# Normed rows kept in natural order; TensorE and GpSimd read them with a step of eight

## What is computed

```
x  = x + g1 * (merged @ w_out)                        # out-projection and residual
h2 = rms_norm(x, norm2_g) * (1.0 + sc2) + sh2         # the normed rows of this case
logits = h2 @ w_router + b_router                     # 32 experts, the best 4 of each token
act = clamp/SwiGLU(h2[tokens of e] @ w_gu[e] + b_gu[e])
y[tokens of e] += weight * (act @ w_down[e] + b_down[e])
x  = x + g2 * y ;  out = rms_norm(x, final_g)
```

## Time and profile before

| | |
|---|---|
| median of 3 executions | 937.23 us (936.38 to 937.92) |
| the profiled execution's own time | 932.74 us |
| its span, first to last instruction | 931.0 us |
| TensorE busy | 895.7 us (96%) |
| TensorE weight loads | 525.3 us (56%) |
| VectorE, ScalarE, GpSimd busy | 454.4, 180.2, 250.0 us |
| mean granted clock of TensorE | 0.994 |
| DMA | 283.75 MB, mean 305 GB/s |

### The profile page before, as it was taken

The page is one execution under the profiler, slowest core; times in us unless marked ns, Lnnn a source line. Parts: engine busy times, 40 slices in busy tenths (PEclk is TensorE's granted clock), DMA queues, the critical chain, the costliest instruction groups (busy, mean ns, idle before and its releaser), DMA issues.

```text
span 931.0 us, 22683 instructions
## 1 busy us (share of the span) xinstructions
PE 895.7 (96%) x10115; PEld 525.3 (56%) x10115; DVE 454.4 (49%) x946; ACT 180.2 (19%) x361; POOL 250.0 (27%) x248
## 2 busy tenths in 40 slices
PE   3999999999999998989999999999999999999994
PEld 2676756766788755755545454544545454544551
DVE  0389967544633556754352534344352534344355
ACT  6344454544322414100000000000000000000012
POOL 2333952202400003223223131323223131323102
PEclk9999999999999999999999999999999999999998
DMA  9937554305422967679999999999999999999965
GB/s 322 366 130 271 181 173 157 123 1 198 175 96 79 408 259 293 257 301 354 375 407 390 407 399 402 404 399 407 394 409 395 409 397 407 404 402 408 391 246 195
DMA packets 64124, 283.75 MB, mean 305 GB/s; under 512 B 7428, under 2 KB 9052, under 8 KB 39448
## 3 DMA queue, kind: packets, MB, share of 16 engines
q1 hardware_dynamic: 53528, 257.93, 69.8%
q0 software_dynamic: 10496, 24.32, 9.3%
HBM read 271.83 MB, written 18.50 MB: 312 GB/s over the span
## 4 chain that ended last, share of the span: by engine, by line
PE 84%; DVE 9%; ACT 3%; DMA 2%; issue 1%; SPq 0%; DVEq 0%; ACTq 0%; POOLq 0%
PE ps L1859 36%; PE ps L1578 16%; PE ps L1882 12%; PE ps L1872 6%; PE ps L1813 2%; DVE small L1157 2%; DVE top L1156 2%; PE ps L1632 2%; PE ps L1718 2%; PE ps L1853 2%; PE ps L1599 1%; DMA moe_rows<-X 1%; PE ps L1733 1%; DVE small L1142 1%; DMA X<-in_x_dram 1%
## 5 line engine op out<-in xcount | busy, mean ns | idle before, releaser
L1354 DVE TENSOR_SCALAR mix<-ps 128x384 f32<-128x384 f32 x32 | 17.9, 558 | 280.1 <-ACT attn L1019 280.1
L753 POOL DMA_INDIRECT moe_rows<-mix,idx x31 | 45.9, 1482 | 345.6 <-DVE mix L1412 345.6
L1578 PE MATMUL ps<-h_hi,wb_hl 128*128 128x512 f32 x384 | 125.5, 400 | 0.0
L1019 ACT ACTIVATE attn<-ps 128x384 f32<-128x384 f32 x32 | 15.7, 491 | 493.2 <-PE ps L1859 493.2
L747 POOL DMA_INDIRECT apad<-h_rows,idx x93 | 97.3, 1046 | 50.6 <-issue 27.7
L1578 PEld LDWEIGHTS ps<-h_hi,wb_hl 128*128 128x128 f32 x384 | 72.1, 188 | 20.8 <-issue 3.9
L1859 PE MATMUL ps<-ring,mix 128*32 128x256 f32 x1440 | 80.0, 379 | 0.0
L1859 PE MATMUL ps<-ring,uvp 128*32 128x256 f32 x1344 | 76.3, 383 | 0.0
L1578 PE MATMUL ps<-h_lo,wb_hl 128*128 128x512 f32 x192 | 74.8, 390 | 0.0
L1404 DVE SCALAR_TENSOR_TENSOR mix<-ps,WC,attn 32x256 f32<-32x256 f32 x128 | 61.6, 481 | 3.8 <-PE ps L1872 1.4
L1859 PEld LDWEIGHTS ps<-ring,mix 128*32 128x32 f32 x1440 | 43.0, 110 | 33.1
(11 more groups left out here) (312 smaller groups left out, 1346.7 us busy)
## 6 DMA issues: line engine op xcount, KB each, us to landing
ring<-in_w_gu_dram SPq DMA_DIRECT2D x58, 1024.0 KB, 23.8
ring<-in_w_down_dram SPq DMA_DIRECT2D x30, 1024.0 KB, 25.7
ring<-in_w_ada_dram SPq DMA_DIRECT2D x12, 2048.0 KB, 11.2
area_b<-in_w_gu_dram SPq DMA_DIRECT2D x17, 1024.0 KB, 18.9
hT<-in_w_gu_dram SPq DMA_DIRECT2D x17, 1024.0 KB, 22.9
area_a<-in_w_gu_dram SPq DMA_DIRECT2D x15, 1024.0 KB, 23.7
X<-in_w_gu_dram SPq DMA_DIRECT2D x14, 1024.0 KB, 26.1
ring<-in_w_in_dram SPq DMA_DIRECT2D x6, 2048.0 KB, 9.1
```

What stands on the lines that cost most here:

```text
L753: pool.indirect_dma_start(out=y_dram, in_=Y[0:slots, b, :], in_offset=None, out_offset=bass.IndirectOffsetOnAxis(ap=which, axis=0), bounds ...
L1578: last = mm(out_, a, b, start=(n == 0 and start_), stop=(n == len(pairs) - 1))
```

## The change

The normed rows are left in the order of X. VectorE's two operations are both in plain order, `first` moves to another tile, and the readers take the step of eight: TensorE's transposes and its product for expert 0 take every eighth element of a row as a block of weights, and GpSimd's copy reads with the same step. Chunk 2's normed row lies in `uvp` and no longer in X, chunk 3's still in `apad`; both are made in place, with no use of the scratch tile. The wait for `y_begun` remains for chunks 0 and 1 and is gone for chunk 2.

```diff
-        h2 = [X[:, ch, :] for ch in range(C - 1)] + [apad_flat[:, PG * (PAD + T) - D:PG * (PAD + T)]]
+        h2 = [X[:, 0, :], X[:, 1, :], uvp[:, :, :].rearrange("p a t -> p (a t)"),
+              apad_flat[:, PG * (PAD + T) - D:PG * (PAD + T)]]
+        h2_block = [t.rearrange("p (q k) -> p k q", k=KD) for t in h2]
...
-        first = natural[:, 0:C * slots].rearrange("p (c s) -> p c s", c=C)
+        first = mix[:, 3072:3072 + C * slots].rearrange("p (c s) -> p c s", c=C)
...
                 nc.gpsimd.tensor_copy(staged[ch % 2].rearrange("p (a k f) -> p k a f", a=NQ, k=KD),
-                                      h2[ch].rearrange("p (k a f) -> p k a f", a=NQ, k=KD)).then_inc(staged_ok, 1)
+                                      h2[ch].rearrange("p (a f k) -> p k a f", a=NQ, k=KD)).then_inc(staged_ok, 1)
...
-            def by_k(row):
-                return row.rearrange("p (q k) -> p k q", k=KD)
...
             def h2_rows(ch):
                 dve.wait_ge(ss3_ok, ch + 1)
                 link(v.reciprocal(rstd3[:, ch:ch + 1], ss3[:, ch:ch + 1]))
-                link(v.scalar_tensor_tensor(out=natural, in0=X[:, ch, :], scalar=rstd3[:, ch:ch + 1], in1=A2b,
+                scaled = natural if ch < 2 else h2[ch]
+                if ch == C - 1:
+                    dve.wait_ge(xg_clear, 1)
+                link(v.scalar_tensor_tensor(out=scaled, in0=X[:, ch, :], scalar=rstd3[:, ch:ch + 1], in1=A2b,
                                             op0=ALU.mult, op1=ALU.mult))
-                if ch < C - 1:
+                if ch < 2:
                     dve.wait_ge(y_begun[ch], 16)
-                else:
-                    dve.wait_ge(xg_clear, 1)
-                v.tensor_tensor(h2[ch].rearrange("p (k q) -> p k q", k=KD), by_k(natural), by_k(sh2b),
-                                ALU.add).then_inc(h2_ok, 1)
+                v.tensor_tensor(h2[ch], scaled, sh2b, ALU.add).then_inc(h2_ok, 1)
...
                     for k in range(4):
-                        at = (4 * half + k) * P
-                        last = nc.tensor.transpose(b_[:, k * P:(k + 1) * P], h2[ch][:, at:at + P], ident[:, :])
+                        last = nc.tensor.transpose(b_[:, k * P:(k + 1) * P], h2_block[ch][:, 4 * half + k, :], ident[:, :])
...
-                    last = mm(ps[:, 4 + k // 4, (k % 4) * P:(k % 4) * P + slots], h2[ch][:, k * P:(k + 1) * P], first[:, ch, :],
+                    last = mm(ps[:, 4 + k // 4, (k % 4) * P:(k % 4) * P + slots], h2_block[ch][:, k, :], first[:, ch, :],
```

## The result

The changed kernel takes 947.55 us (median of 4 executions, 946.77 to 947.86), the kernel before on the same chip 936.81 us (4 executions, 934.65 to 937.92). The ratio is 1.0119, with a 95% interval of 1.0103 to 1.0134: slower, by about 11.1 us by the ratio and 10.7 by the two medians. The profiled execution took 947.52 us; its span is 945.4 us, for 931.0 before.

The account below looks back on a forecast made before the run. TensorE, 84% of the chain, was taken as the bound, with expert 0's product at the pace of weight loads. 0.1 + 0.4 + 0.34 + 6.5 = +7.4 us took the median from 937.23 to 944.6 us, range 934.2 to 947.5.

Parts of the forecast that it names:

- The product, +6.5 us: Expert 0's product (L1951): 64 weight loads at 0.102 us more each, all on the chain, +6.5 us.
- The estimate from VectorE's row: TensorE's stepped weight loads: VectorE's strided addition, 0.80 ns more per element, carried over as 0.102 us more per load.
- the bounds given (0 to 0.14): TensorE's stepped weight loads: extra per load from 0 up to 0.14 us, a column at the strided addition's 1.99 ns.
- The transposes, +0.1 us after eating 2.19, +0.4 and +0.34 for chunk 3: TensorE before the routers and product: stepped transposes eat VectorE's 2.19 us, +0.1 us; chunk 3 adds +0.4 and +0.34.
- a load costs the same at any step: Rival, chance 0.38: L1951 and the transposes pay 0 for the step; 2.19 us gain remains, median 935.0 us.
- the smaller price (0.056 us): Rival, chance 0.17: stepped loads cost 0.056 us more each, as VectorE's 12-byte row; sum +3.0, median 940.2 us.
- VectorE's addition, 0.81 us per chunk: VectorE's addition at L1289: plain order takes 1.226 us for 2.04, 0.81 us less per chunk.
- The floor of the out-projection: Before x1_half(3): the last right half's end at 357.94 us limits VectorE's 2.67 us gain to 2.19.
- GpSimd's longer copy beside VectorE: GpSimd's stepped staging copy could slow the VectorE operation beside it by 0 to 0.5 us; taken as 0.
- The two rows used as bounds: VectorE's slowest plain addition, 1.717 us for 1.226, and GpSimd's copy in runs of three, 1512/384 = 3.9 ns per element.
- The clock, no charge: TensorE's granted clock, 1.00 in these stages: a fall was named as making the forecast wrong, without a price.
- The experts' pace: Experts from 420 to 888 us: stay at TensorE's 16.1 us each, with some 15 us in hand for weight loads.

Follow-up runs that it names:

- experiment 5: Kernel before, with expert 0's product reading its weights at a step of four elements (16 bytes): 979.87 us for 969.47, one execution.
- experiment 6: Kernel before, with expert 0's product reading its weights at a step of two elements (8 bytes): 971.01 us for 969.47, one execution.
- Experiment 9: Changed kernel with GpSimd's staging copy reading in plain order: 945.87 us for the kernel before's 936.19, ratio 1.0105.
- experiment 1: Kernel before, with only expert 0's product reading its weights at the step of eight: 948.56 us for 936.17, ratio 1.0132.
- experiment 4: Changed kernel with expert 0's product taking its weights in plain blocks of 128: 935.59 us, ratio 0.999 to the kernel before.
- experiment 8: Changed kernel with a useless bf16 matmul behind each of the product's 32 matmuls: 979.29 us for the kernel before's 969.47, ratio 1.0117.
- experiment 7: Changed kernel with its transposes made as float32 products with the identity, still at the step of eight: 987.88 us for the kernel before's 969.47, one execution.

## Why the prediction was wrong

The forecast was 944.6 us, slower by 7.4; it came out slower by 11, at 947.55 us, just above the range's end of 947.5. The side was right, and the main place too: the product of expert 0. What failed are four terms: the product's price was too small, the transposes' too large, and GpSimd's copy beside VectorE and the clock were put at nothing and cost 1.7 and 4.0 us. By its steps:

- **The product, +6.5 us.** Measured +8.20. The estimate from VectorE's row, 0.102 us more per load, was too small: it is 15.58/64 - 7.38/64 = 0.128 us. The value lies inside the bounds given (0 to 0.14), close to the upper one, which was left out of the range. (At that bound 64 x 0.14 is 9.0 us and not 9.2, which makes 948.4 us.) The form was wrong too: a price per column that grows with the step is not what experiments 5 and 6 show.
- **The transposes, +0.1 us after eating 2.19, +0.4 and +0.34 for chunk 3.** Measured nothing, 0 from the first router to the product. The same price was put on all 96 loads as if a load were a load; 16 transposes take 1.96 us for 1.91. The rival "a load costs the same at any step" holds for 32 loads and falls for 64, and the smaller price (0.056 us) falls for both.
- **VectorE's addition, 0.81 us per chunk.** Right: 1.23 us for 2.04. Experiment 9 shows the sum without the floor, 2.66 us for the 2.67 worked out. The floor of the out-projection didn't bind there, since the first DMA landed later in that execution than in that of the earlier trace rows.
- **GpSimd's longer copy beside VectorE, taken as 0, bounded by 0.5 us.** This step failed. The copy's length (2.05 us, within 1.05 to 4.0) was rightly hidden as to its DMA and the gathers, but it held VectorE's scaling up by 0.94 us in each of two chunks. Experiment 9 takes that away and gains 1.67 us. I had asked when the copy ends and not what it holds up meanwhile. The two rows used as bounds were one such meeting: the addition of 1.717 us for 1.226 ran from 238.97 us, beside GpSimd's cast (L703) and then its copy L705 from 239.67, the row of 1512 ns. In the other traces, where the two don't meet, they take 1.23 us and 622 to 631 ns. So the 4.0 us were no rate of a copy, and 0.5 us was no bound: the rows at 114 us, shown above, lose 2.16 and 0.60 us.
- **The clock, no charge.** This step failed too. It is named at the end as what would make the forecast wrong, without a price. It is worth +2.77 + 1.21 = 4.0 us behind the product. Experiments 1, 4 and 8 show that it comes with the slow product and goes without its step or with a filler between; experiment 7 shows that slow loads need not bring it. Here the longer stage wasn't only longer: what TensorE did after it started at the 1.2 GHz level.
- **The experts' pace.** Right: 467.73 us for 467.70. The 29.5 us of the earlier trace rows are of the stretch from 640 to 720 us; from 720 to 800 the same loads took 30.3, which leaves the cover of some 15 us as it is.

The errors had both signs: the product's 1.7 us and the clock's 4.0 us missing; 0.84 us for transposes too much; and before the router a gain of 0.99 us, where 2.19 were thought gained and eaten. In sum -0.99 + 8.20 + 4.0 = +11.2 us. That the result lies so close to the range's end is luck: 5.7 us too little and 1.8 too much partly cancelled.

On the rules: of the Trainium skill's page "TensorE: Matmul & The Clock Gate", section "LDWEIGHTS (loading the stationary operand)", columns/1.2 ns agrees with the plain loads (107 for 115 ns) and with the transposes at any step, and not with the product at 16 and 32 bytes, where 128 columns take 240 ns. The Trainium skill's page "Advanced Engine Details and Errata", section "Memory Cachelines", asks for two hits on a line of 16 bytes. With a step of 8 bytes there are two and the load costs 0.122 us; with 16 bytes there is one and it costs 0.239. For the product this case agrees with it; the transposes' pace doesn't show it.

## What to carry to other kernels

Where a stage runs at the pace of weight loads of float32 products, keep the weights' elements at most 8 bytes apart, or move the reordering to where it is hidden (here, the order of a DMA that loads weights). When an operation off the chain becomes longer, look at which instruction of a neighbour that is on the chain falls beside it, as well as at when it ends. And give the clock a price where a stage of TensorE would come to run at the pace of its loads: here the rows behind it paid 4.0 us, though experiment 7 shows such a stretch that kept it.

## What the runs showed of the hardware

- The weight load of a float32 product of 128 columns: 0.115 us in plain order, 0.122 at a step of 8 bytes, 0.239 at 16 and 0.243 at 32 bytes. Transposes of the same blocks pass in 0.119 us without the step and 0.122 us with it, though their load rows are 141 and 193 ns.
- TensorE showed busy 100% in the product in each kernel, and where its loads were slow the granted clock fell to 0.50, 4.6 us after its start in the changed kernel, 5.6 us in experiment 1, 5.4 in experiment 5 and 3.8 in experiment 9, and stayed there for about 17 us. A filler matmul behind each kept it at 1.00 (experiment 8), and it stayed at 1.00 through 11.3 us of slow loads in experiment 7. The loads' pace was the same on both levels.
- GpSimd's copy of 1024 float32 elements took 1.05 us in plain order and 2.05 with the step of eight. Beside the latter VectorE's scaling nearly stood still until the copy was over (2.2 for 1.29 us). In experiment 9 copy and scaling overlap by only 0.14 us, so no run shows this scaling beside a plain copy for longer. But GpSimd additions without a step held a VectorE operation of 0.29 us for 2.45 and 0.89 us, until they ended: it takes a meeting, and the step brought one about by making the copy longer.
- VectorE's transposes of gathered rows took 1.62 us with the step for 0.96 without.
